# A decoder layer on one NeuronCore: both input norms ahead of the first projection, the bonus products moved into the first inversion, the group norm's roots and reciprocals gathered in one tile

## The reference, cut to what matters

```python
u = rmsnorm(x, norm1_g)                       # x * rsqrt(mean(x*x) + 1e-6) * g
# RWKV branch, 8 heads of 64 channels
kk = kk / max(sqrt(sum(kk*kk)), 1e-12)        # per head
y, wkv_new = rwkv_recurrence(r, decay, k_mod, v, kk, a, wkv0)
mu  = mean(y);  var = mean((y - mu)**2)       # group norm, per token and head
yn  = (y - mu) * rsqrt(var + 64e-5) * lnx_w + lnx_b
bonus = sum(r * k_mod * r_k) * v              # per head
ya  = (yn + bonus) * g
branch_a = ya @ w_branch_a
merged = sigmoid(gA) * branch_a + sigmoid(gB) * branch_b
x = x + merged @ w_out
x = x + hier_moe(rmsnorm(x, norm2_g))         # top-1 group, top-2 experts, SwiGLU
```

## Time and profile before

| | us |
|---|---|
| median of 3 runs (943.31 to 944.09) | 943.62 |
| profiled execution | 941.25 |
| its span in the trace | 939.6 |
| TensorE busy | 861.0 (92%) |
| VectorE busy | 388.5 (41%) |
| ScalarE busy | 216.1 (23%) |

### The profile page before, as it was taken

How to read it: one execution, slowest core, us unless ns; L and a number is a source line. 1 busy time by engine, 2 the same in 40 slices (tenths; PEclk the granted TensorE clock), 3 DMA queues, 4 the chain that set the end, 5 groups by cost and what they waited for, 6 DMA issues and landing times. The chain is left out here.

```text
span 939.6 us, 20334 instructions
## 1 busy us (share of the span) xinstructions
PE 861.0 (92%) x8922; PEld 606.6 (65%) x8922; DVE 388.5 (41%) x746; ACT 216.1 (23%) x437; POOL 37.6 (4%) x34
## 2 busy tenths in 40 slices
PE   5999999999989789999989989999799918999994
PEld 4877777788866567777767767777687703333321
DVE  4443433428955635444533315434621162111125
ACT  2111011023153222231222124222002050111134
POOL 0000000000000000000000000000000000222213
PEclk9999999999999979999999989998999958999998
DMA  9211111311311101111111200108271178999975
GB/s 357 89 52 45 45 45 46 142 48 68 112 46 55 46 12 37 36 36 37 37 36 47 92 24 25 48 2 287 88 287 50 45 251 359 399 395 390 392 235 211
DMA packets 27015, 118.82 MB, mean 126 GB/s; under 512 B 5344, under 2 KB 7648, under 8 KB 22064
## 3 DMA queue, kind: packets, MB, share of 16 engines
q1 hardware_dynamic: 22608, 106.57, 29.8%
q0 software_dynamic: 4320, 10.95, 4.0%
HBM read 104.24 MB, written 18.05 MB: 130 GB/s over the span
## 5 line engine op out<-in xcount | busy, mean ns | idle before, releaser
L877 PE MATMUL psum<-arena 128*128 128x268 f32 x1600 | 405.7, 403 | 14.5 <-DVE arena L1422 8.0
L877 PEld LDWEIGHTS psum<-arena 128*128 128x128 f32 x1600 | 300.6, 194 | 86.7 <-DVE arena L1422 10.7
L1422 DVE TENSOR_TENSOR arena<-psum,arena 128x256 f32<-128x256 f32 (+7 forms) x230 | 99.5, 438 | 285.0 <-PE psum L1175 56.9
L1236 ACT ACTIVATE arena<-psum 128x268 f32<-128x268 f32 (+9 forms) x181 | 72.5, 410 | 473.1 <-PE psum L877 292.5
L1422 DVE TENSOR_TENSOR arena<-arena 128x268 f32<-128x268 f32 (+11 forms) x203 | 102.1, 503 | 54.3 <-ACT arena L1236 43.6
L1175 PE MATMUL psum<-arena 128*128 128x268 f32 x384 | 91.1, 394 | 6.2 <-DVE arena L1422 6.2
L1958 PE MATMUL psum<-arena 128*32 128x512 f32 (+1 forms) x640 | 88.2, 615 | 5.2 <-DVE arena L2111 5.2
L1175 PEld LDWEIGHTS psum<-arena 128*128 128x128 f32 x384 | 72.6, 192 | 21.4 <-issue 6.7
L2111 DVE TENSOR_TENSOR arena<-psum,arena 128x256 f32<-128x256 f32 (+1 forms) x36 | 24.1, 692 | 110.6 <-ACT arena L2025 106.1
L1958 PEld LDWEIGHTS psum<-arena 128*32 128x32 f32 (+1 forms) x640 | 25.6, 118 | 64.4 <-issue 60.2
L1425 DVE SCALAR_TENSOR_TENSOR arena<-arena 128x268 f32<-128x268 f32 (+6 forms) x101 | 48.2, 477 | 3.1 <-DVE arena L1422 0.2
(11 more groups left out here) (183 smaller groups left out, 693.8 us busy)
## 6 DMA issues: line engine op xcount, KB each, us to landing
arena<-in_w_gu SPq DMA_DIRECT2D x16, 2048.0 KB, 22.8
arena<-in_w_in SPq DMA_DIRECT2D x46, 512.0 KB, 3.5
arena<-in_w_dn SPq DMA_DIRECT2D x16, 1024.0 KB, 20.9
arena<-in_w_out SPq DMA_DIRECT2D x2, 2048.0 KB, 11.6
arena<-in_x SPq DMA_DIRECT2D x8, 268.0 KB, 4.9
arena<-in_x SPq DMA_DIRECT2D x1, 2144.0 KB, 9.2
arena<-in_rets SPq DMA_DIRECT2D x1, 2048.0 KB, 16.5
out_rets<-arena SPq DMA_DIRECT2D x1, 2048.0 KB, 6.5
```

The source lines that it names most:

```text
L877: last = mm(ps, wt[:, i % NW, k, :], rhs[:, k, cols(hf)], start=(k == 0), stop=(k == nk - 1))
L1236: run(nc.scalar.activation(out, in_, fn, **kw), s)
L1422: run(v.tensor_tensor(out, a, b, op), s)
```

## The change

- Head: SP sends both halves of x first; the first constants shrink by the matrix of ones, which DVE writes with a memset. TensorE no longer waits for the constants before the first norm. Both norms' matmuls come before projection tile 14, and ACT and DVE square both halves before the first root and reciprocal.
- Key norms: both halves of head pair 3 come together behind projection (2, 0); LoRA w and a of head pair 0 come together behind projection (2, 1).
- The sample tokens' decay exponential (`wsmp`) moves from `sm_a` to `wk_e` of chunk 0.
- Bonus: the `j_bon` pairs enter the queue only from the first chunk's inversion on.
- Group norm: `VAR` groups the units: 0 to 3, 4 and 5, 6. `j_var` of a group writes the variance of all eight heads into one 128-row tile (16 rows each, four matmuls of 32 columns of `bones`), so one root and two reciprocals serve the group; `j_bc` spreads a head's row over its 64 channels again (matmuls of 64 columns), and DVE multiplies from PSUM, in place of `ln_w`. Means of units 4 and 5 are taken before the last chunk is done.
- Experts: for the last pass DVE takes `rows_in` ahead of `hidden` of the pass before.

```diff
-    s = [("sq", 0), ("j_norm", 0, 0), ("sq", 1)]
+    s = [("sq", 0), ("sq", 1), ("j_norm", 0, 0), ("j_norm", 0, 1)]
...
-            put((4, 5, 7, 8)[p], hf, ("j_kkn", p, hf))
-            put(8 + p, hf, ("j_lora", "w", p, hf), ("j_lora", "a", p, hf))
+            put((4, 5, 7, 8)[p], hf if p < 3 else 0, ("j_kkn", p, hf))
+            put(8 + p, hf if p else 1, ("j_lora", "w", p, hf), ("j_lora", "a", p, hf))
...
-    bonus = [("j_bon", p, hf) for p in range(NP) for hf in range(2)]
+    bonus = []
...
+        if c == -1:
+            bonus += [("j_bon", p, hf) for p in range(NP) for hf in range(2)]
...
+        if c == len(CHUNKS) - 2:
+            side[0:0] = [("j_mean", 4), ("j_mean", 5)]
+            side += norms(1)
...
             half_of_x(0)
+            half_of_x(1)
             sp.dma_start(con[:, 0:NFIRST], I["con"][:, 0:NFIRST]).then_inc(s_load, 16)
...
-            pe.wait_ge(s_load, 32)
+            pe.wait_ge(s_set, 1)
...
                 elif kind == "j_var":
+                    g = step[1]
+                    n0, n1, c0, c1 = VAR[g]
+                    ps = open_job(step)
+                    pe.wait_ge(s_vsd, n1)
+                    if g == 2:
+                        last = mm(job_ps(step, NP * (c1 - c0)), bones, un(tmp, n0), start=True, stop=True)
+                    else:
+                        few = bones.rearrange("t (a b) -> t a b", b=4)[:, :, 0]
+                        for p in range(NP):
+                            last = mm(ps[H * p:H * p + H, 0:c1 - c0], few, tmp[:, p, c0:c1], start=True, stop=True)
+                    last.then_inc(s_job, 1)
+                elif kind == "j_bc":
                     n = step[1]
+                    p0, p1, c0, c1 = UNITS[n]
                     open_job(step)
-                    pe.wait_ge(s_vsd, n + 1)
-                    mm(un_ps(n)[1], bones, un(tmp, n), start=True, stop=True).then_inc(s_job, 1)
+                    pe.wait_ge(s_rc, 1 if n < NP else 2)
+                    for p in range(p0, p1):
+                        for a in range(2):
+                            row = H * p + 16 * a
+                            last = mm(un_ps(kind, n)[64 * a:64 * a + 64, p - p0, :],
+                                      ident[:, row:row + 1].broadcast_to([P, 64]), tmp[:, 0, c0:c1],
+                                      start=True, stop=True)
+                    last.then_inc(s_job, 1)
...
+                    if c == 0:
+                        f(wsmp, ly[:, :, TP:T], ACT.Exp, scale=-DECAY, s=s_sw)
...
-                    if i == 0:
-                        job_read(dve, ("j_var", n))
-                    if n < 6:
-                        k = PIECES[n] // (p1 - p0)
-                        o = c0 + i % k * (c1 - c0) // k
-                        x = tmp[:, p0 + i // k, o:o + (c1 - c0) // k]
-                    else:
-                        x = un(tmp, n)
-                    run(v.reciprocal(x, x))
+                    job_done(dve, step)
+                    for p in range(p0, p1):
+                        y = ly[:, p, c0:c1]
+                        run(v.scalar_tensor_tensor(y, y, vv("lnw", p), un_ps(kind, n)[:, p - p0, :], ALU.mult, ALU.mult),
+                            free if p == p1 - 1 else None)
...
                     for i in range(NPASS - 1):
+                        if i == NPASS - 2:
+                            rows_in(i + 1)
                         hidden(i)
```

More of the change, by code:

```diff
@@ L83 @@
 NKEEP = CON["perm"][0]
-NFIRST = CON["ones"][0] + P
+NFIRST = CON["ones"][0]
 def constants():
@@ L277, in order, with norms @@
                                                       ("j_sy", p), ("sm_d", p)]
-    def norms(n):
-        p0, p1, _, _ = UNITS[n]
-        return [("ln_r", n, i) for i in range(PIECES[n])] + [(k, n, p) for p in range(p0, p1 if n < 6 else 1)
-                                                               for k in ("ln_w", "ln_b")] + [("ln_g", n)]
+    def norms(g):
+        n0, n1, _, _ = VAR[g]
+        out = [("j_var", g)] + [("ln_r", g, i) for i in range(2 if g < 2 else 1)]
+        for n in range(n0, n1):
+            p0, p1, _, _ = UNITS[n]
+            out += [("j_bc", n)] if g < 2 else [("ln_w", n, p0)]
+            out += [("ln_b", n, p) for p in range(p0, p1 if g < 2 else 1)] + [("ln_g", n)]
+        return out
     s += [("wk_e", 0)] + prep(0, ("wk_p", 0), ("wk_p", 1), ("wk_p", 2), ("wk_p", 3), ("wk_d", 0), ("wk_d", 1)) + take(6)
@@ L301, in order @@
             assert not side, side
-            s += [("j_var", n) for n in range(NP)]
-            side += [x for n in range(NP) for x in norms(n)]
+            s += [("j_var", 0)]
+            side += norms(0)[1:]
+        if c == len(CHUNKS) - 2:
+            side[0:0] = [("j_mean", 4), ("j_mean", 5)]
+            side += norms(1)
         s += [("wk_t", c + 1, 8)] + prep(c + 2, ("wk_d", 0)) + take(1)
@@ L308, in order @@
     r, sa, _, _, st = solved(len(CHUNKS) - 1)
-    assert not any(x[0].startswith("j_") for x in side), side
-    side += [("j_mean", 4), ("j_mean", 5)]
     s += r + take(2, 2) + sa + [("wk_sp", len(CHUNKS) - 1)] + take(2, 2) + st
-    side += [("j_mean", 6), ("j_var", 4), ("j_var", 5)] + norms(4) + [("j_var", 6)] + norms(5) + norms(6)
+    side += [("j_mean", 6)] + norms(2)
     ba = [("j_ba", m, 0) for m in range(8)]
-    cost = {"ln_r": 0.9, "ln_w": 0.55, "ln_b": 0.55, "ln_g": 0.6, "j_mean": 0.6, "j_var": 0.1}
+    cost = {"ln_r": 0.9, "ln_w": 0.55, "ln_b": 0.55, "ln_g": 0.6, "j_mean": 0.6, "j_var": 0.1, "j_bc": 1.0}
     credit = 0.0
@@ L325, in order @@
             s.append(side.pop(0))
+            if s[-1][0].startswith("j_"):
+                break
     s += side
@@ L550, in hybrid_step @@
         s_vsd = sem("s_vsd")
+        s_rc = sem("s_rc")
         s_ya = sem("s_ya")
@@ L1363, in _ @@
                     job_done(act, step)
-                    f(un(tmp, step[1]), un_ps(step[1])[1], ACT.Sqrt, scale=1.0 / 64, bias=lnx_eps, s=free)
+                    n0, _, c0, c1 = VAR[step[1]]
+                    if step[1] == 2:
+                        f(un(tmp, n0), job_ps(step, NP * (c1 - c0)).rearrange("t (p k) -> t p k", p=NP), ACT.Sqrt,
+                          scale=1.0 / 64, bias=lnx_eps, s=free)
+                    else:
+                        f(tmp[:, 0, c0:c1], job_ps(step, c1 - c0), ACT.Sqrt, scale=1.0 / 64, bias=lnx_eps, s=free)
                 elif kind == "x2":
@@ L1429, in ts @@
                     else v.tensor_scalar(out, a, s1, None, op0), s)
-            run(v.memset(eps, EPS), s_eps)
+            run(v.memset(ones, 1.0), s_set)
+            run(v.memset(eps, EPS), s_set)
             run(v.memset(lnx_eps, LNX_EPS))
@@ L1688, in _ @@
                     job_done(dve, step)
-                    stt(un(ly, n), un_ps(n)[0], -1.0 / 64, un(ly, n), ALU.mult, ALU.add, s=free)
+                    stt(un(ly, n), un_ps(kind, n), -1.0 / 64, un(ly, n), ALU.mult, ALU.add, s=free)
                 elif kind == "ln_r":
-                    _, n, i = step
-                    p0, p1, c0, c1 = UNITS[n]
-                    if i == 0:
-                        job_read(dve, ("j_var", n))
-                    if n < 6:
-                        k = PIECES[n] // (p1 - p0)
-                        o = c0 + i % k * (c1 - c0) // k
-                        x = tmp[:, p0 + i // k, o:o + (c1 - c0) // k]
-                    else:
-                        x = un(tmp, n)
-                    run(v.reciprocal(x, x))
+                    _, g, i = step
+                    n0, _, c0, c1 = VAR[g]
+                    if i == 0:
+                        job_read(dve, ("j_var", g))
+                    if g == 2:
+                        run(v.reciprocal(un(tmp, n0), un(tmp, n0)))
+                    else:
+                        x = tmp[:, 0, c0 + i * (c1 - c0) // 2:c0 + (i + 1) * (c1 - c0) // 2]
+                        run(v.reciprocal(x, x), s_rc if i else None)
+                elif kind == "j_bc":
+                    n = step[1]
+                    p0, p1, c0, c1 = UNITS[n]
+                    job_done(dve, step)
[3 more added lines that the diff above has]
+                            free if p == p1 - 1 else None)
                 elif kind in ("ln_w", "ln_b"):
```

31 lines of the change are left out of this document (14 added, 17 removed).

## The result

| | before | after |
|---|---|---|
| median of 4 runs, us | 943.86 (943.31 to 944.76) | 917.43 (916.77 to 918.78) |
| profiled execution: time, span, mean granted clock | 941.25, 939.6, 0.960 | 917.91, 916.2, 0.973 |

The ratio is 0.9721, with a 95% interval of 0.9704 to 0.9738: 26.4 us less by the medians, 23.3 between the two profiled executions. I had said 923.0, in 914.5 to 931: the time lies in that range, and just under the 918 to 928 to which I had given 0.57.

The account below looks back on a forecast made before the run. The mixer was taken as a queue of TensorE work, losing time where it idles or runs at the lower clock. Gains 6.5 + 1.6 + 8.7 + 0.3 + 3.5 = 20.6 gave 920.65 profiled, 923.0 as median, range 914.5 to 931.

Parts of the forecast that it names:

- The three main waits: TensorE's waits for vectors in the head (7.4 us), VectorE at the recurrence's start (8.02) and in the group norm's tail (5.0).
- head: Start of kernel: x first and norms ahead of tile 14, starting at about 13.1; gain 6.5 us, bounds 3 to 8.
- key norms, LoRA: Projections: waits of 1.63 and 1.93 go, one of about 1.9 comes; gain 1.6 us, bounds 0 and 3.6.
- recurrence: Start of recurrence: `wk_a` 10.8 earlier, exponential 4.0, less bonus, bank and clock costs; gain 8.7 us, bounds 4.5 and 13.
- group norm, all units: Variances and broadcasts of units 0 to 3 gain 0.3 us, units 4 and 5 with the end 3.5.
- experts: Last pass's gate products lose a 2.3 us wait, but the late rows' gather sets the end: nothing, at most 0.5.
- clock in units and tail: Group norm units and tail: no clock gain was included in the forecast sum.
- the other pairs wait for banks: Recurrence: bonus pairs after the first two wait because VectorE has the inversion's products ahead; cost 1.5 us.
- My own reading against it: Key norms: the old 2.23 us wait held two table loads and an exponential, so no extra 1.4 us drain.
- The rule of the Trainium skill that I had weighed: Group norm broadcasts: changing tiling drains TensorE; the prediction kept the trace's 0.16 us per change, 0.8 in all.
- everything goes well: Rival: clock holds in head and recurrence, no bank waits, tail gains more; 27.0 us gain, 916.6, chance 0.08.
- The rival of a low clock over the tail: Rival: narrow matmuls spread the low clock from the first `j_bc` on; 17.8 us slower, 961, chance 0.02.

Follow-up runs that it names:

- run 1: The head's edit alone (x halves first, ones set on chip, both norms ahead of the first projection), on the kernel before: 936.12 us, ratio 0.9916.
- run 5: The changed kernel with key norms and low-rank jobs placed as before: 919.22 us.
- run 3: The changed kernel with the bonus products queued first again, ahead of the inversion, sample exponential left in its new place: 920.64 us.
- run 4: The changed kernel with the sample tokens' exponential back in its old place, the first sample step: median 923.89 us, six runs from 918.47 to 928.75.
- run 2: The group norm's edit alone, on the kernel before: 937.15 us, ratio 0.9943.
- run 11: The changed kernel with the last expert pass's operands made behind the sums of the pass before again: 917.21 us, ratio 0.9732.
- run 6: The changed kernel with no short job (bonus pair, sample product, mean) at the first place behind a chunk's exponentials: 907.98 us, ratio 0.9619.
- Run 9: The changed kernel with each group norm broadcast as one full-width matmul in place of two of 64 columns: 918.36 us.
- run 8: The changed kernel with useless matmuls (18, 12, 12 and 2 of 240 columns) in TensorE's four waits of the routing stage: 921.42 us.
- run 10: The changed kernel with fewer useless matmuls (20, 3, 9 and 2 of 240 columns) in the routing stage's waits: 916.30 us, ratio 0.9723.
- run 7: The changed kernel with useless matmuls in five of TensorE's waits in the mixer: 914.34 us, ratio 0.9691.

## Why the prediction was right

The three main waits went as said, and the time fell in the stated range. But the sum is near for a reason that was not in it: the terms I had priced gave 16.4 of their 20.6, and a term that I had put at nothing, the clock of units and tail, gave 6.9. By the milestones, with the clock set apart:

| step | predicted | measured in the trace | by runs |
|---|---|---|---|
| head | 6.5 | 7.0 | 7.0 (run 1) |
| key norms, LoRA | 1.6 | -0.1: 1.6 of waiting gained, 1.7 lost to the clock | 1.8 (run 5) |
| recurrence | 8.7 | 6.85 | 3.2 (run 3), 4.3 to 6.5 (run 4) |
| group norm, all units | 3.8 | 3.3 | 6.0 with the clock (run 2) |
| experts | 0 | -0.7 | 0 (run 11) |
| clock in units and tail | 0 | 6.9 | |
| sum | 20.6 | 23.3 | |

*Head.* The gain is right, its course only half. The norms' matmuls lasted until 14.66, since TensorE follows x as it lands, and tile 14 started there and not at 13.1; but it had no gap ahead of it and no low clock, and took 4.2 and not 5.7. The two errors cancel, which is luck. Half 1 was normed in time, as said. (The bytes were summed a little short: x half 0, constants and vectors are 1.32 MB, not 1.29, and 2.36 after; it shifts the landing by 0.1 us.)

*Key norms.* Two waits became one of 1.93, as said. That the clock fell behind the one and not behind the two was not foreseen: the four LoRA records and the projection behind them took 1.7 more, 1.3 of it in the projection.

*Recurrence.* `wk_a` came 10.8 earlier, to the tenth, behind 2.40 us of idle time (2.3 predicted). The clock did not fall there (1.9 gained), and TensorE waited 0.8 for a bank that VectorE reads, where 0.8 and 1.5 had been put in. The failed step is "the other pairs wait for banks, because VectorE has the inversion's products ahead of them, 1.5": the third pair waited 2.91 for ScalarE. It stands behind the projection job that follows the exponentials of chunk 2; ScalarE reads that job's bank only after two table loads and two exponentials. The low clock behind it cost 1.4 more, and some 0.9 of the rest is not traced to a row. Run 3 shows the price (6.9 for two pairs), run 6 the cause. ScalarE in after, between the end of its chunk work and the reading of that bank:

```profile
363.85 1.28 ACT L1262 ACT_TABLE_LOAD   x1
365.14 0.73 ACT L1262 ACTIVATE arena<-arena 128x256 f32<-128x256 f32 x2
365.89 1.28 ACT L1262 ACT_TABLE_LOAD   x1
367.19 0.40 ACT L1262 ACTIVATE arena<-psum 128x268 f32<-128x268 f32 x1
```

Each load is followed by its activation within 0.02 us. The Trainium skill, "ScalarE: Activation LUTs", section "What ACT_TABLE_LOAD costs", adds a drain of some 1380 ns to the load; neither these rows nor the new wait of 1.93 show one. My own reading against it was careless: the wait of 2.23 in before did not hold two loads and an exponential. They ran from 344.19 to 347.02, 2.83 us, and TensorE began to wait at 345.2; but they too stand within 0.02 us of each other, so the conclusion stays. The trace of before had two waits of the same making, at the mean and at the sample product, and I had taken them for a fixed cost instead of asking what the new job would find in such a place.

*Group norm.* Variances: 2.9 gained, 3.0 expected. Broadcasts of units 0 to 3 with what they cost their neighbours: 3.0 lost, against 1.9 and 0.8 for tilings. The tail: 3.4 against 3.5. From the second half of the last projection (623.27) to the first `j_ba` of half 1 (about 647.6, by its reading at 649.74) it is 24.3, to the tenth what I had walked, with waits of 0.76, 0.82 and 0.95. Run 9 shows that nothing is won by avoiding the change of tiling. The rule of the Trainium skill that I had weighed ("TensorEngine Tiling (Array Packing)", section "Key Properties": a change of mode drains the engine) stands at no more than 0.05 us a broadcast over a matmul of full width, 1.71 against 1.66.

*The clock.* This is the term that was missing: the prediction lets the clock vary in the head and at `wk_a` and puts it at nothing behind. Four times in units and tail after paid less for it than before: 1.5 behind the wait at 468 us (481 in before), 1.1 behind the third mean, 2.9 in the last projections, 1.4 behind 669 of before. Run 2 says that the third is not the group norm's doing, since it stays with that edit alone, and that the fourth is, since it goes. The first and the third at least are chance in this pair of traces: run 11 has both again in the same mixer, at 3.2 and 3.4 us of TensorE's time by clock and busy time (before: 1.7 and 3.4). Over whole sets of runs the changed kernel did gain by the clock: after's four runs had mean clocks of 0.972 and 0.973, and five runs of run 11's kernel 0.967 to 0.976, where the 42 later runs of before lay between 0.956 and 0.965. How much of that belongs to which edit stays open. Of the rivals, "everything goes well" had the size (916.6) and of its reasons only the clock at `wk_a`: the bank waits and the tail gave next to nothing extra. The rival of a low clock over the tail did not come: after's trace has none there, and run 11's one stretch.

*Experts.* The gate products lost their wait, then TensorE stood 1.89 us for VectorE ahead of 895.58 in its place, the first pass took 9.98 where before's took 8.60, at the low clock both times, and the gather set the end:

```profile
876.40 6.76 DMA x_rows<-arena,ids
886.83 10.78 DMA arena<-x_rows,ids
```

The earlier trace rows has the gather at 910.63 with 10.30.

*The medians.* Before's profiled run was 2.6 under its median, after's 0.5 over. I had carried the first difference over to after; the forecast from the profile alone, 920.65, was nearer.

## To carry over

Before a short job is moved behind a step of ScalarE, count what ScalarE has queued ahead of the read that frees its bank: two table loads and two exponentials were not covered by a short job here, and were by a projection job (run 6). Price an edit at the full clock first, and keep the low clock as a term of its own, since it can be as large as the edit (7 of 23 us here). Where an idle time can't be filled with work that is needed, a few matmuls of no use, shorter than the wait, are worth a run (2 to 3 us in the mixer here). Before a slower time is put down to an edit, look where in the trace the time was lost: in run 8 most of it lay ahead of the edit.

## What the hardware showed unexpectedly

- **Runs of one kernel differ mostly by the clock.** Eleven runs of before, in one set, took 939.16 to 945.43 us with mean granted clocks from 0.964 to 0.957; span times clock is 902.6 with a standard deviation of 0.8 (the clock is given to three places, which is 0.5 us). Before and after differ by 25 us in span but by 11.9 in that product (902.6 and 890.7). The product also discounts low clock in idle time (of before's 324 to 336, clock 0.57, TensorE was busy for 6.1 us only), so it understates what the edits gained in waiting.
- **The same wait lowers the clock in one run and not in the next.** The 2.40 us ahead of the first inversion left the clock at 1.00 in after and at 0.56 in run 4, whose row of 32 records took 3.07 against 1.98. Four traces share after's mixer (after, runs 8, 10 and 11); their low stretches there cost 5.0, 9.9, 6.8 and 11.8 us of TensorE's time, by the busy time and the clock of slices of 1 us.
- **The clock also falls without a wait.** In the stretch of run 6 below TensorE was busy throughout. The matmuls turn slow in the middle of products with 16 rows, as they did in before ahead of 636, and did not in after.

```profile
607.05 0.27 PE L1153 MATMUL psum<-arena 16*64 16x16 f32 x4
...
608.28 0.39 PE L1149 MATMUL psum<-arena 16*64 16x16 f32 x4
```

```profile
607.00:615.00 8.00, 8.00 (x52) 5.73 (x52) 0.65 (x2) 0.63 (x3) 0.00 (x0) 0.57 0.59 137
```

- **Filling waits went with a higher clock** (0.975 to 0.978 in run 7, 0.979 to 0.984 in run 10), at no cost seen while the filler is shorter than the wait. Where it was not (run 8), TensorE came 3.7 us later to its next step than in after or run 10 (10.4 against 6.7 us behind the routing matmuls), and had won all of it back, and 0.7 more, by the end of the first pass. What decides in a given run whether the clock falls stays open.
- **The last scatter varies** by 3 us though the instruction is the same: 6.76, 7.84 and 9.66 in after and runs 6 and 10.
